# Moving a latent attention's per-head queries, keys and values behind the gate's weight panels, with queries and keys passed through DRAM

## What is computed

```
q = (rms_norm(c_q, q_a_norm) @ w_uq).reshape(B, L, 8, 96)
kv = (rms_norm(c_kv, kv_a_norm) @ w_ukv).reshape(B, L, 8, 128)
k_nope, v = kv[..., :64], kv[..., 64:]
k = concatenate([k_nope, broadcast(k_rope)], -1)
q, k = rms_norm(q, q_norm), rms_norm(k, k_norm)
q, k = ... with apply_rope on the last 32 of 96
s = q k^T / sqrt(96), masked by chunks; softmax; o = probs v; out = o * silu(z)
```

## Time and profile before

| | |
|---|---|
| device time, median of 3 runs (lowest, highest) | 2217.54 us (2216.91, 2222.42) |
| profiled execution: its time, its span | 2216.88 us, 2214.8 us |
| mean granted PE clock | 0.962 of full |
| busy share of the span: PE, DVE, ACT, POOL | 93%, 47%, 32%, 18% |
| DMA traffic | 122.30 MB, mean 55 GB/s |
| latent stage's gate panels | 1796.0 to 1850.0 us |
| heads stage, then head 0's preparation, then the first scores | from 1858.9, from 1922.5, at 1934.7 us |

### The profile page before, as it was taken

How to read it: one execution, slowest core, us unless ns; L and a number is a source line. 1 busy time by engine, 2 the same in 40 slices (tenths; PEclk the granted TensorE clock), 3 DMA queues, 4 the chain that set the end, 5 groups by cost and what they waited for, 6 DMA issues and landing times.

```text
span 2214.8 us, 24695 instructions
## 1 busy us (share of the span) xinstructions
PE 2048.9 (93%) x9965; PEld 1671.8 (75%) x9965; DVE 1042.4 (47%) x1700; ACT 697.9 (32%) x1203; POOL 389.0 (18%) x435
## 2 busy tenths in 40 slices
PE   7979799969999999999999999997989997599999
PEld 6767588747877888888888888776978886377677
DVE  4666734645455333333333336437345324766541
ACT  4444122234443221212212214433111114555521
POOL 3152202630030000000000003342323114301100
PEclk9999899969999999999999999998999998799999
DMA  4134232121111111111111112113111111000023
GB/s 139 39 94 125 83 87 78 55 79 46 48 53 46 50 48 48 48 48 48 48 48 48 48 48 61 37 47 119 35 39 29 54 39 43 4 1 1 29 77 95
DMA packets 175914, 122.30 MB, mean 55 GB/s; under 512 B 17785, under 2 KB 163449, under 8 KB 175801
## 3 DMA queue, kind: packets, MB, share of 16 engines
q1 hardware_dynamic: 175800, 120.73, 18.2%
HBM read 100.78 MB, written 19.92 MB: 55 GB/s over the span
## 4 chain that ended last, share of the span: by engine, by line
PE 78%; DVE 12%; ACT 4%; issue 2%; POOL 2%; DMA 1%; SPq 0%; ACTq 0%; DVEq 0%; POOLq 0%
PE ps L310 21%; PE ps L311 20%; PE ps L312 20%; PE ps L323 3%; PE ps L2558 3%; PE ps L514 2%; PE ps L1171 1%; DVE wlo L297 1%; PE ps L2547 1%; PE ps L2548 1%; DVE fm L907 1%; PE ps L2549 1%; DVE xl L1435 1%; PE ps L2488 1%; PE ps L1155 1%
## 5 line engine op out<-in xcount | busy, mean ns | idle before, releaser
L310 PE MATMUL ps<-xh,whi 128*128 128x512 f32 (+2 forms) x1728 | 693.3, 401 | 36.0 <-DVE wlo L297 18.1
L311 PE MATMUL ps<-xl,whi 128*128 128x512 f32 (+2 forms) x1728 | 673.7, 390 | 0.0
L312 PE MATMUL ps<-xh,wlo 128*128 128x512 f32 (+2 forms) x1728 | 670.6, 388 | 0.0
L310 PEld LDWEIGHTS ps<-xh,whi 128*128 128x128 f32 x1728 | 331.5, 192 | 111.9 <-issue 25.4
L312 PEld LDWEIGHTS ps<-xh,wlo 128*128 128x128 f32 x1728 | 330.5, 191 | 66.2
L311 PEld LDWEIGHTS ps<-xl,whi 128*128 128x128 f32 x1728 | 331.0, 192 | 62.2 <-issue 3.1
L291 ACT ACTIVATE whi<-wraw 128x1024 fp32r<-128x1024 f32 (+2 forms) x151 | 146.9, 973 | 362.6 <-PE ps L312 349.9
L297 DVE TENSOR_TENSOR wlo<-wraw,whi 128x1024 fp32r<-128x1024 f32 (+2 forms) x151 | 193.3, 1280 | 113.7 <-ACT whi L291 113.6
L310 PE MATMUL ps<-ffh,whi 128*128 128x512 f32 x512 | 199.4, 389 | 0.0
L311 PE MATMUL ps<-ffl,whi 128*128 128x512 f32 x512 | 199.3, 389 | 0.0
L312 PE MATMUL ps<-ffh,wlo 128*128 128x512 f32 x512 | 199.2, 389 | 0.0
(11 more groups left out here) (434 smaller groups left out, 2603.0 us busy)
## 6 DMA issues: line engine op xcount, KB each, us to landing
wraw<-w_in SPq DMA_DIRECT2D x47, 512.0 KB, 3.8
wraw<-w_up SPq DMA_DIRECT2D x32, 512.0 KB, 4.0
wraw<-w_down SPq DMA_DIRECT2D x32, 512.0 KB, 3.4
xt<-x SPq DMA_DIRECT2D x8, 512.0 KB, 6.9
wraw<-w_o SPq DMA_DIRECT2D x16, 256.0 KB, 2.9
xr<-x SPq DMA_DIRECT2D x8, 512.0 KB, 4.8
wraw<-w_ple_gate SPq DMA_DIRECT2D x8, 512.0 KB, 4.2
h_d<-hT SPq DMA_DIRECT2D x8, 512.0 KB, 3.4
```

The source lines that it names most:

```text
L310: pe.matmul(out, h, xh[:, k, c0:c1_], start=(k == 0), stop=False)
L311: pe.matmul(out, h, xl[:, k, c0:c1_], start=False, stop=False)
L312: mm = pe.matmul(out, l, xh[:, k, c0:c1_], start=False, stop=(k == nk - 1))
```

## The change

It does the following.

1. The gate panels mz0 to mz3 are cut into eight halves. `pe_dense` calls `behind` after every input block k of 0 to 7, and `slot_at` names the blocks with a slot behind them: 2, 5, 7 in halves 0 to 2; 1, 3, 5, 7 in halves 3 to 5; 1 to 7 in halves 6 and 7.
2. The first 21 slots hold the 17 items in their old step order (slot n: step 3 of item n-3, step 2 of n-2, step 1 of n-1, step 0 of n). The last 14 hold head 0's preparation, queries before keys. The stage of its own for the items and the loop's h = -1 are gone. ACT, DVE and POOL follow the same slots; DVE evicts each half of z after that half's slots. Items use the four "misc" PSUM banks, two per item.
3. The splits of c_q, c_kv and w_uq move to the panels c1, c2 and kr, that of w_ukv to the start of mz1; sumq moves from behind mz1 to behind c2, sumkv and the k_rope transposes into half 0.
4. `tqm` and `ktm` give way to a ring of five tiles `qk`. When an item is finished SP stores its tile to DRAM (`q_d`, `k_d`). When all 17 have landed, SP loads head 0's columns of all blocks into `qhd` and `khd` (1024 pieces of 384 bytes for the queries, as many for the keys); head 1's follow once mz3 is done, since its buffers lie where the input of the panels was; each later head's when the head two before it has been transposed.
5. `yc` and `ro` are stored to DRAM at the start of the stage and come back into `yb` and `rb` after head 0's loads.

The core of the diff (buffer addresses, and bodies that only move, are left out):

```
+    yc_d = nc.dram_tensor("yc_d", (128, 2 * T), F32).ap()
+    ro_d = nc.dram_tensor("ro_d", (128, 256 * NB), F32).ap()
+    q_d = nc.dram_tensor("q_d", (NB, 128, 768), F32).ap()
+    k_d = nc.dram_tensor("k_d", (NB + 1, 128, 768), F32).ap()
...
+    n_items = 2 * NB + 1
+    head_slots = [[(n - lag, lag) for lag in (3, 2, 1, 0) if 0 <= n - lag < n_items] for n in range(n_items + 3)]
+    slot_at = [(2, 5, 7)] * 3 + [(1, 3, 5, 7)] * 3 + [tuple(range(1, 8))] * 2
+    first_slot = [sum(len(x) for x in slot_at[:n]) for n in range(9)]
+    n_head_slots = first_slot[6]
+    assert n_head_slots >= len(head_slots)
...
+    def in_slots(half, heads, first):
+        for n in range(first_slot[half], first_slot[half + 1]):
+            for m, s in head_slots[n] if n < n_head_slots else ():
+                heads(m, s)
+            for step in prepare[n - n_head_slots] if n >= n_head_slots else ():
+                first(*step)
...
+        def behind(half):
+            k = [0]
+            def call():
+                if half == 0 and k[0] == 1:
+                    p = take(w, "misc", ("sumkv",), (act_la, ("sumkv meta",)))
+                    w.wait_ge(*pool_la.at("fsq", 2))
+                    for x in range(NB + 1):
+                        n, cs = key_block(x)
+                        t = pe.matmul(p[0:n, x:x + 1], fsq[0][:, cs], ones[:, 0:1], start=True, stop=True)
+                    t.then_inc(*pe_la.up("sumkv"))
...
+                if k[0] in slot_at[half]:
+                    n = first_slot[half] + slot_at[half].index(k[0])
+                    if n < n_head_slots:
+                        for m, s in head_slots[n]:
+                            heads_pe(pe, w, m, s)
+                    else:
+                        for step in prepare[n - n_head_slots]:
+                            prepare_pe(pe, w, 0, *step)
+                k[0] += 1
...
+            if (kind, j) == ("c", 1):
+                w.wait_ge(*ld_uq.at())
+                w.wait_ge(*st_h1.end())
+                act.activation(uqH[:], uqr[:], ACT.Copy).then_inc(*act_la.up("uq high"))
+            if (kind, j) == ("c", 2):
+                for j_ in range(2):
+                    w.wait_ge(*dve_la.at("ev", "c", j_, HALF2))
+                    act.activation(cqH[:, j_, :], fcq[j_][:, NMETA:T2], ACT.Copy, scale=V("gqa")[:, j_:j_ + 1]).then_inc(*act_la.up("cq high", j_))
...
+            if j == 1:
+                w.wait_ge(*ld_uk.at())
+                act.activation(ukH[:], ukr[:], ACT.Copy).then_inc(*act_la.up("uk high"))
+            for hf in range(2):
+                in_slots(2 * j + hf, lambda m, s: heads_act(act, w, m, s), lambda *step: prepare_act(act, w, 0, *step))
         silu(3)
-        w.wait_ge(*pe_la.at("mz", 3, HALF2))
-        for j in range(2):
...
+                w.wait_ge(*st_y.end())
+                w.wait_ge(*act_la.at("uq high"))
+                dve.tensor_tensor(uqL[:], uqr[:], uqH[:].bitcast(F32), ALU.subtract).then_inc(*dve_la.up("uq low"))
...
-        w.wait_ge(*dve_la.at("uq low"))
-        dve.tensor_tensor(ukL[:], ukr[:], ukH[:].bitcast(F32), ALU.subtract).then_inc(*dve_la.up("uk low"))
+            if j == 1:
+                for n_, bs in ((128, slice(0, NB)), (NMETA, slice(NB, NB + 1))):
+                    w.wait_ge(*pool_la.at("krs", n_))
+                    dve.tensor_reduce(kr2[0:n_, bs], krs[0:n_, bs, :], AX.X, ALU.add).then_inc(*dve_la.up("kr2", n_))
+                w.wait_ge(*act_la.at("uk high"))
+                dve.tensor_tensor(ukL[:], ukr[:], ukH[:].bitcast(F32), ALU.subtract).then_inc(*dve_la.up("uk low"))
+            for hf in range(2):
+                in_slots(2 * j + hf, lambda m, s: heads_dve(dve, w, m, s), lambda *step: prepare_dve(dve, w, 0, *step))
+                scaled_dve(dve, w, (kind, j), REAL2[hf:hf + 1], dst, off, pe_la, dve_la)
     def latent_pool(pool, w):
...
+    def heads_act(act, w, m, s):
+        t = qk[m % 5]
+        if s == 0 and m > 1:
+            w.wait_ge(*dve_la.at("sum", m - 2))
+        if s == 0 and m > 4:
+            w.wait_ge(*st_qk[m % 5].at(m - 5))
...
+    def heads_sp(sp, w, m):
+        if m < NB:
+            w.wait_ge(*pool_la.at("q rope", m))
+            sp.dma_start(q_d[m], qk[m % 5][:]).then_inc(*st_qk[m % 5].up(m))
+        else:
+            n = key_block(m - NB)[0]
+            w.wait_ge(*dve_la.at("k normed", m - NB))
+            sp.dma_start(k_d[m - NB, 0:n], qk[m % 5][0:n, :]).then_inc(*st_qk[m % 5].up(m))
+    def head_sp(sp, w, h):
+        r, fs = h % 2, slice(96 * h, 96 * h + 96)
+        if h > 1:
+            w.wait_ge(*pe_at.at("kT", h - 2, 2))
+            w.wait_ge(*pe_at.at("qT", h - 2, 1))
+        sp.dma_start(qhd[r][:, :, 0:96], q_d[:, :, fs].rearrange("b p d -> p b d")).then_inc(*ld_q[r].up(h))
+        sp.dma_start(khd[r][:, 0:NB, :], k_d[0:NB, :, fs].rearrange("b p d -> p b d")).then_inc(*ld_k[r].up(h, "all"))
+        sp.dma_start(khd[r][0:NMETA, NB, :], k_d[NB, 0:NMETA, fs]).then_inc(*ld_k[r].up(h, "meta"))
...
-    prepare = [[("kT", 0)], [("kT", 1)], [("kT", 2), ("qT", 0)], [("qT", 1)]] + [
+    prepare = [[("qT", 0)], [("qT", 1)], [("kT", 0)], [("kT", 1), ("kT", 2)]] + [
...
         if what == "kT":
             p = take(w, "max", ("kT", h, t), (dve_at, ("kl", h, t)))
-            for x in key_tile(t)[1]:
-                w.wait_ge(*dve_la.at("k normed", x))
-            pe_turn(pe, [(p[0:96, 128 * j:128 * j + n_keys(x)], ktm[0:n_keys(x), x, 96 * h:96 * h + 96]) for j, x in enumerate(key_tile(t)[1])]
+            w.wait_ge(*ld_k[r].at(h, "meta"))
+            pe_turn(pe, [(p[0:96, 128 * j:128 * j + n_keys(x)], khd[r][0:n_keys(x), x, :]) for j, x in enumerate(key_tile(t)[1])]
                     ).then_inc(*pe_at.up("kT", h, t))
         elif what == "qT":
             p = take(w, "max", ("qT", h, t), (dve_at, ("ql", h, t)))
-            w.wait_ge(*pool_la.at("q rope", 4 * t + 3))
-            w.wait_ge(*pool_la.at("q pad"))
-            pe_turn(pe, [(p[0:104, 128 * j:128 * j + 128], tqm[:, 768 * (4 * t + j) + 96 * h:768 * (4 * t + j) + 96 * h + 104]) for j in range(4)]
-                    ).then_inc(*pe_at.up("qT", h, t))
+            w.wait_ge(*pool_la.at("q pad", r))
+            w.wait_ge(*ld_q[r].at(h))
+            pe_turn(pe, [(p[0:104, 128 * j:128 * j + 128], qhd[r][:, 4 * t + j, :]) for j in range(4)]).then_inc(*pe_at.up("qT", h, t))
         elif what == "max":
...
         sp_weights(sp, w, IN20 + 16 + 2)
         for sem in (pe_i2, act_i2, dve_i2, pool_i2):
             w.wait_ge(*sem.end())
+        sp.dma_start(uqr[:], ap["w_uq"].rearrange("(k p) n -> p k n", p=128)).then_inc(*ld_uq.up())
+        sp.dma_start(ro_d, ro[:].rearrange("p b d -> p (b d)")).then_inc(*st_y.up("ro"))
+        sp.dma_start(yc_d, yc[:].rearrange("p c t -> p (c t)")).then_inc(*st_y.up("yc"))
         sp.dma_start(c3[:], ap["c3"]).then_inc(*ld_c3.up())
-        sp_weights(sp, w, IN20 + 16 + 6 + 3)
-        w.wait_ge(*dve_la.at("mkv meta"))
-        sp.dma_start(uqr[:], ap["w_uq"].rearrange("(k p) n -> p k n", p=128)).then_inc(*ld_uq.up())
-        sp_weights(sp, w, OUT0 - 1 + 3)
-        w.wait_ge(*pe_la.at("mz", 3, HALF2))
+        sp_weights(sp, w, IN20 + 16 + 6)
+        w.wait_ge(*dve_la.at("ck low"))
+        w.wait_ge(*pool_la.at("fsq", 2))
         sp.dma_start(ukr[:], ap["w_ukv"]).then_inc(*ld_uk.up())
-        w.wait_ge(*pe_la.at("q", NB - 1, 1))
+        sp_weights(sp, w, IN20 + 16 + 7)
+        w.wait_ge(*dve_la.at("uq low"))
+        for m in range(n_items):
+            heads_sp(sp, w, m)
+            if m in (7, 13):
+                sp_weights(sp, w, OUT0 + m // 8)
         sp.dma_start(ak[96:AUG, :], ap["kaug"]).then_inc(*ld_aug.up("k"))
         sp.dma_start(aq[96:AUG, :], ap["qaug"]).then_inc(*ld_aug.up("q"))
+        for sem in st_qk:
+            w.wait_ge(*sem.end())
+        head_sp(sp, w, 0)
+        w.wait_ge(*st_y.end())
+        sp.dma_start(yb[:].rearrange("p c t -> p (c t)"), yc_d).then_inc(*ld_y.up("yc"))
+        sp.dma_start(rb[:].rearrange("p b d -> p (b d)"), ro_d).then_inc(*ld_y.up("ro"))
+        w.wait_ge(*pe_la.at("mz", 3, HALF2))
+        for h in range(1, 8):
+            head_sp(sp, w, h)
```

439 lines of the change are left out of this document (209 added, 230 removed).

## The result

The changed kernel took **2192.27 us** (median of 4 runs, 2190.02 to 2193.57), the kernel before 2218.57 us (4 runs, 2216.91 to 2222.42) on the same chip: ratio 0.9878, interval [0.9861, 0.9895], 26.3 us less. The forecast was 2194, its range 2176 to 2208. The profiled execution took 2190.02 us, with a span of 2188.1. Its last eviction ahead of the changed stage (fcq of c2) lies 1.0 us later than before's. That difference arose ahead of the stage, 0.4 us in the first 640 us of the program and 0.5 between 1510 and 1533, so times of after are to be read 1.0 later than the forecast's.

What follows compares the result with a forecast made beforehand. PE had no panel for 84.7 us between the last gate product and head 0's first scores. Following the engine chain through six steps put PE's 1934.7 position at 1912.0, 22.7 us earlier: 2216.88 became 2194 us, range 2176 to 2208.

Steps and rivals of the forecast that it cites:

- Sumq moved, 6.7: Sumq, moved behind c2, costs the same 6.7 us as before, now ahead of mz0, which starts at 1802.7.
- Halves 0 and 1 are PE's, to 1829.8: In mz0's two halves PE sets the pace: panels 11.1, query items 13.0, sumkv 2.0, k_rope transposes 1.0 us.
- The ring, 52.0 us: After mz0, ACT and DVE's item cycle paces: 3.45 us per item plus panel boundaries; last key block ready at 1881.8.
- No order of slots shortens that ring: ACT and DVE need 3.45 us per key item in any order, since the root stands ahead of the next copies.
- Round trip 7.6: Last tile's store to DRAM 3.4, head 0's load 3.8, issuing 0.4 us; PE gets the queries at 1889.4.
- The rival of slow small pieces: Loads of 384-byte pieces take twice 3.8 us, two exposed: 2202, with late tiles up to 2208; chance 0.21 for 2202 to 2210.
- 18.4 for the rest of the panels and the preparation: From queries' arrival to first scores: panel 9.7, head 0's preparation 7, low clock 1.7 us; first scores at 1907.8.
- Head 1's load, 4.2: Head 1's loads wait for mz3's last product; PE loses 3.5 us at the query transposes and 0.7 by the clock.
- heads at the same distance as before from head 1 on: Sign of being right: from head 1 on, heads follow each other as far apart as in the kernel before.
- PE's waits for ACT's copies: Sign of being right: PE's "misc" products wait for ACT copies in half 3 or 4, some 5 to 12 us in all.
- The wait at head 0's transposes: Sign at head 0's first query transpose: one PE wait of 7 to 20 us if right, under 5 if wrong.
- go by the row: Table load counted at the profile's 1.28 us without the skill's drain, which at four switches would add 5.5 us, about 2200.

Runs made afterwards that it cites:

- sumq spread: Changed kernel with sumq's 32 one-column products placed four behind each of kr's first eight blocks, instead of one block between c2 and kr: 2188.11 us.
- root last: Changed kernel with ACT doing item n's copies and square ahead of item n-1's square root in each slot: 2187.98 us, ratio 0.9858.
- No cover: Changed kernel with all slots moved behind mz3's last block, so items and head 0's preparation no longer lie over the panels: 2212.46 us, ratio 0.9968.

## Why the prediction was right

1. *Sumq moved, 6.7.* Right in kind, 1.6 too much: it cost 16.53 - 11.46 = 5.07. The products take 3.7, and the low clock behind them the rest (sumq spread).
2. *Halves 0 and 1 are PE's, to 1829.8.* PE has no wait there. mz0's first product starts at 1801.83, and the first one behind q5's item at 1828.32: 26.5 us instead of 27.1.
3. *The ring, 52.0 us.* From 1828.32 to 1880.76 it took 52.4. Key items are 3.45 apart (1851.53, 1854.97, 1858.42). But two reasons in it fell. "No order of slots shortens that ring" is wrong: with the root last the items come in 2.5 us where the tiles allow it. And I summed the boundaries as ACT's line of work, 5.7 and 3.7; they are 7.0 and 3.6, and are set by two chains, ACT's and the one by way of DVE's split, which stands ahead of the sum in DVE's order. The sizes came near because both chains are of about one length. The boundaries are 1.2 us longer in sum than I took and the rest of the step 0.8 shorter, so that it agrees to 0.4 is partly luck. That PE "then stands at the first slot of half 6" is right.
4. *Round trip 7.6.* It took 1886.21 - 1880.76 = 5.45. The last tile is the meta block, 16 rows, and its store landed in 1.7 us instead of 3.4; the load took 3.5 against my 3.8. The rival of slow small pieces falls. The Trainium skill (DMA: Bandwidth & Descriptors, Specifications) puts pieces under 512 B below line rate; here 384 KB in pieces of 384 bytes landed in 3.5 us (the keys behind them in 4.1) and the panels' 512 KB in 3.8. That is 110 KB per us against 135, but the loads also differ in size, so no run here shows by itself that the pieces are slower.
5. *18.4 for the rest of the panels and the preparation.* 18.1.
6. *Head 1's load, 4.2.* It costs 3.4 by taking it away, but against the kernel before only 2.1, since that one lost 1.3 in the same stretch. The other 1.4 of the 3.5 lost behind the first scores were put at nothing: "heads at the same distance as before from head 1 on" is wrong by 0.2 us a head, 1.1 in all, and 0.3 come at the end. That the step misses by only 0.7 is partly luck.

Of the signs, PE's waits for ACT's copies (7.9 us in all) lie in their 5 to 12, and key items, loads, c2 and kr show none of the signs of being wrong. The wait at head 0's transposes, 6.0, lies under the 7 to 20 that were to be right and over the 5 that were to be wrong, and head 1's, 2.8, under its 3 to 4.

The sum of the errors: 1.6 + 0.6 + 2.1 + 0.3 + 0.7 us too much in steps 1, 2, 4, 5 and 6, 0.4 too little in step 3, and 0.2 for mz0's start, which was read from an eviction: 5.1. The 1.0 us by which the execution came late to the stage takes part of it back. Forecast 22.7 less, measured 26.9 in the profiled executions and 26.3 in the medians. No cover shows that the reason at the base of it holds: without the overlap the time is 2212.46. On table switches the trace does not agree with the Trainium skill (ScalarE: Activation LUTs, What ACT_TABLE_LOAD costs), which adds a drain of about 1.38 us to a load. In the changed kernel the load starts 0.02 us behind whi, the silu at 1832.24, 0.01 behind a load of 1.28 us, and the root at mz1/mz2 (1865.47) 0.02 behind the other. The sum was right to go by the row.

## What to carry to other kernels

When elementwise work is laid over a dense stage, cost the places where the stage's own chores (splits, table loads) enter the queues of the helper engines: a split that waits for another engine blocks whatever stands behind it, and one slot later it was free. Two chains of one length hide each other: taking either away brought the last key block 2.1 and 2.6 us forward, both 8.1. A round trip through DRAM can be split by what is ready first: queries ahead of keys gave 1.8 us up to the first scores (and 1.8 behind them for a reason that isn't settled). Then look for the next chain beside it: keys in two loads gave nothing, since the augmented rows came no earlier.
